# A kernel with a mixture of experts on one core: the experts' work moved into the block before it, and the expert rows weighted, gated and added to the residual rows by the scatter

## What is computed

```python
x = x + gt1 * (merged @ w_out)                    # residual rows x1
h2 = rmsnorm(x, norm2_g) * (1.0 + sc2) + sh2
# each row picks one of 4 groups and 2 of the 8 experts in it; weights: (1024, 2)
y = (silu(h2 @ w1[e]) * (h2 @ w3[e])) @ w2[e]     # for each of its 2 experts e
x = x + gt2 * (weights[:, 0] * y_0 + weights[:, 1] * y_1)     # x2
# second block
h = rmsnorm(x, norm_attn_g_2) * (1.0 + sc1) + sh1
proj = h @ w_in_2
```

## Time and profile before

| what | us |
| --- | --- |
| median of 3 runs | 3923.98 |
| lowest and highest run | 3920.57, 3938.64 |
| the profiled execution | 3928.56 |
| its span, first to last instruction | 3926.7 |
| joining, first to last row of TensorE | 993.3 to 1274.0 |
| experts, first to last row of TensorE | 1290.2 to about 2010.3 |
| mixer, from TensorE's first row | 2024.3 |

### The profile page before, as it was taken

How to read it: one execution, slowest core, us unless ns; L and a number is a source line. 1 busy time by engine, 2 the same in 40 slices (tenths; PEclk the granted TensorE clock), 3 DMA queues, 4 the chain that set the end, 5 groups by cost and what they waited for, 6 DMA issues and landing times. The chain is left out here.

```text
span 3926.7 us, 45778 instructions
## 1 busy us (share of the span) xinstructions
PE 3702.7 (94%) x17988; PEld 1967.0 (50%) x17988; DVE 1739.0 (44%) x2939; ACT 950.9 (24%) x1977; POOL 472.1 (12%) x374
## 2 busy tenths in 40 slices
PE   6999998999998799999968999999898999999999
PEld 3554444555454344444434457865655444444444
DVE  2479998655566000000021335546353344333246
ACT  2311111554232122222223212322243311111001
POOL 0032244311000111111110111111000000000000
PEclk8979999999998899999976999999899999999999
DMA  4213232121554789898955213223103111111334
GB/s 174 75 47 121 76 120 80 55 71 35 207 192 155 278 329 340 329 340 329 341 191 178 101 58 99 79 80 101 60 17 116 41 43 43 43 44 49 125 113 158
DMA packets 295129, 533.07 MB, mean 136 GB/s; under 512 B 25236, under 2 KB 104180, under 8 KB 292638
## 3 DMA queue, kind: packets, MB, share of 16 engines
q1 hardware_dynamic: 277214, 480.56, 35.4%
q0 software_dynamic: 13040, 43.55, 2.8%
q10 hardware_dynamic: 4688, 6.36, 0.4%
HBM read 462.68 MB, written 67.73 MB: 135 GB/s over the span
## 5 line engine op out<-in xcount | busy, mean ns | idle before, releaser
L570 PE MATMUL ch_side<-aT,space 128*128 128x512 f32 x896 | 391.6, 596 | 0.0
L1791 DVE TENSOR_SCALAR ex_y<-ex_y,ex_weight 128x1024 f32<-128x1024 f32 x32 | 41.1, 1284 | 639.9 <-PE ex_y L1711 639.9
L570 PEld LDWEIGHTS ch_side<-aT,space 128*128 128x128 f32 x896 | 168.6, 190 | 213.3 <-issue 210.6
L1695 PE MATMUL ex_a<-space,ex_xT 128*128 128x512 f32 x512 | 229.0, 601 | 6.2 <-ACT ex_xT L1762 6.2
L3015 PE MATMUL en_bank<-en_h,en_up 128*128 128x512 f32 x528 | 233.8, 592 | 0.0
L1711 PE MATMUL ex_y<-aT,ex_actT 128*128 128x512 f32 x512 | 228.1, 599 | 0.7 <-ACT ex_actT L1774 0.7
L1695 PE MATMUL ex_b<-space,ex_xT 128*128 128x512 f32 x512 | 225.0, 592 | 0.0
L2177 PE MATMUL mx_duo<-mx_chunks,mx_region 128*128 128x512 f32 x384 | 183.6, 634 | 0.0
L695 DVE MAX8 ch_best<-ch_score 128x8 f32<-128x384 f32 (+5 forms) x192 | 171.6, 894 | 6.1
L696 DVE MATCH_REPLACE8 ch_score<-ch_best,ch_score 128x384 f32<-128x384 f32 (+5 forms) x192 | 168.1, 875 | 0.0
L1695 PEld LDWEIGHTS ex_a<-space,ex_xT 128*128 128x128 f32 x512 | 98.5, 193 | 130.7 <-issue 130.7
(11 more groups left out here) (536 smaller groups left out, 5884.1 us busy)
## 6 DMA issues: line engine op xcount, KB each, us to landing
space<-exp_w SPq DMA_DIRECT2D x64, 2048.0 KB, 11.8
aT<-exp_w SPq DMA_DIRECT2D x32, 2048.0 KB, 14.0
en_up<-w_down SPq DMA_DIRECT2D x132, 256.0 KB, 3.7
space<-w_ada SPq DMA_DIRECT2D x12, 2048.0 KB, 8.1
mx_x<-proj_padded SPq DMA_DIRECT2D x96, 256.0 KB, 3.6
space<-ada_w SPq DMA_DIRECT2D x8, 2048.0 KB, 8.8
aT<-w_in SPq DMA_DIRECT2D x7, 2048.0 KB, 8.7
en_up<-w_gate SPq DMA_DIRECT2D x22, 512.0 KB, 4.8
```

The lines of the kernel that those rows point to most:

```text
L570: last = nc.tensor.matmul(side_ps[i % 2][:, 0:width], hT[:, k, t * P:(t + 1) * P], by[:, k, 0:width], start=k == 0, stop=k == KD - 1)
L1695: last = nc.tensor.matmul(ps[:, :], xT[b][:, k, :], w13[b][s][:, k, :], start=k == 0, stop=k == KD - 1)
L1791: nc.vector.tensor_scalar(y[b][:, :], y_ps[:, :], weight[b][:, :], None, ALU.mult).then_inc(y_ready, 1)
```

## The change

The functions of `experts` become parts of `joining`'s block: its tiles take memory that `joining` has done with, its PSUM tiles become pairs of `joining`'s banks, and each engine goes on to its experts' work when the new semaphore `listed` says that the experts' list is written. There is no stage boundary between the two any more; `mixer` gets a barrier of all engines at its start. GpSimd also waits for `entered` and `moe_w_stored`. ScalarE issues the store of the weights; the second, small store of it is gone. The first block's `xT` is written half by ScalarE and half by VectorE. gt2 is spread over the partitions at the end of joining (`row2`, `then.gate`), VectorE weights and gates a result in one instruction, and the scatter adds the rows to the x1 rows in HBM (`compute_op=ALU.add`); x2 is the same memory as x1, with 128 more rows for unused places. In `mixer` all work on `ey`, the sums and the stores of x2 are gone. For row tile 1 of joining, VectorE's `weigh("first", 1)` now stands behind `mix(1, 1)`, not ahead of it.

```diff
@@ joining
-        bank = [ctx.enter_context(nc.psum_tensor(f"jn_bank{b}", [P, CH], F32)) for b in range(8)]
+        duo = [ctx.enter_context(nc.psum_tensor(f"jn_duo{b}", [P, 2, CH], F32)) for b in range(4)]
+        bank = [duo[b // 2][:, b % 2, :] for b in range(8)]
...
+        then = experts(nc, g, ctx, space, dsa, aT, duo, gain)
@@ sync
             sp.dma_start(w13[0][1], g.d["exp_w3"][0, 0].rearrange("(k p) f -> p k f", p=P)).then_inc(g.w3_loaded[0], 16)
+            sp.wait_ge(listed, 1)
+            then.sync(sp)
@@ tensor
+            for k in range(KD):
+                column = g.modT[:, 5 * KD + k:5 * KD + k + 1].broadcast_to([P, P])
+                last = nc.tensor.matmul(by_tile(bank[k // 4])[:, k % 4, :], column, g.ident[:, :], start=True, stop=True)
+            last.then_inc(row2, 1)
+            pe.wait_ge(listed, 1)
+            then.tensor(pe)
@@ scalar
+            act.wait_ge(row2, 1)
+            for n in range(2):
+                last = nc.scalar.copy(then.gate[:, n * CH:(n + 1) * CH], bank[n])
+            last.then_inc(then.gate_set, 1)
+            act.wait_ge(weighted, 1)
+            act.dma_start(g.d["moe_w"].rearrange("(t p j) n -> p t (j n)", p=P, j=2), g.weight[:, :, :]).then_inc(moe_w_stored, 16)
+            act.wait_ge(listed, 1)
+            then.scalar(act)
@@ gpsimd
-            pool.wait_ge(weighted, 1)
-            pool.dma_start(g.d["moe_w"][0:SLOTS, :].rearrange("(t p j) n -> p t (j n)", p=P, j=2), g.weight[:, :, :]).then_inc(g.moe_w_stored, 16)
-            pool.dma_start(g.d["moe_w"][SLOTS:SLOTS + P, :], g.eps[:, :]).then_inc(g.moe_w_stored, 16)
+            pool.wait_ge(listed, 1)
+            pool.wait_ge(entered, 1)
+            pool.wait_ge(moe_w_stored, 16)
+            then.gpsimd(pool)
@@ vector
                 mix(t, 0)
-                if t >= 1:
+                if t >= 2:
                     weigh("first", t)
                 mix(t, 1)
-                if t == 0:
+                if t < 2:
                     weigh("first", t)
...
-            chain(V.tensor_copy(g.experts[:, :], line[:, :]))
+            V.tensor_copy(g.experts[:, :], line[:, :]).then_inc(listed, 1)
...
+            chain(TS(g.entries[:, :, 1], target[:, :], -1.0, 0.0, ALU.add, ALU.max))
             chain(TS(blank[:, :], codes, 0.0, empty[:, 0:1], ALU.is_equal, ALU.mult))
-            chain(V.scalar_tensor_tensor(g.entries[:, :, 1], target[:, :], -1.0, blank[:, :], ALU.add, ALU.add))
+            TT(g.entries[:, :, 2], token[:, :], blank[:, :], ALU.add).then_inc(entered, 1)
...
+            dve.wait_ge(listed, 1)
+            then.vector(dve)
@@ experts, now functions that joining calls; what differs in them
+                pool.indirect_dma_start(g.d["x1_rows"], bass.IndirectOffsetOnAxis(entry[b][:, 2:3].bitcast(U32), 0), y[b][:, :], None,
+                                        compute_op=ALU.add).then_inc(scattered[b], 16)
...
+        pe.wait_ge(then.gate_set, 1)
+        pe.wait_ge(x_ready, 1)
+        pe.wait_ge(first_ready, 1)
+        up(0, 0, a_ps, a_done)
...
+        copy_x(1, 0, KD // 2)
...
+        dve.wait_ge(x_flipped, 1)
+        for k in range(KD // 2):
+            last = nc.vector.tensor_scalar(xT[0][:, k, :], x_ps[:, k, :], gain[:, k:k + 1], shift[:, k:k + 1], ALU.mult, ALU.add)
+        last.then_inc(first_ready, 1)
+        dve.wait_ge(then.gate_set, 1)
...
+                nc.vector.scalar_tensor_tensor(y[b][:, :], y_ps, weight[b][:, :], then.gate[:, :], ALU.mult, ALU.mult).then_inc(y_ready, 1)
@@ mixer
+    nc.all_engine_barrier()
...
-                y_v = g.d["moe_y"][0:SLOTS, :].rearrange("(t p j) n -> p t j n", p=P, j=2)
-                for t in range(NT + 2):
+                for t in range(NT):
+                    yield -20.0 if t < 2 else N3_PACE * (t - 2) + 2.0
                     if t >= 2:
-                        yield N3_PACE * (t - 2) - 0.1
-                        sp.wait_ge(combined, t - 1)
-                        sp.dma_start(rows(g.d["x2"])[:, t - 2, :], nx[t % 2]).then_inc(x2_stored[t % 2], 16)
-                    if t < NT:
-                        yield -20.0 if t < 2 else N3_PACE * (t - 2)
-                        sp.dma_start(ey[t % 2], y_v[:, t, :, :]).then_inc(e_loaded[t % 2], 16)
-                        if t >= 2:
-                            yield N3_PACE * (t - 2) + 2.0
-                            sp.wait_ge(n_scaled, t - 1)
-                            sp.wait_ge(x2_stored[t % 2], 16 * (t // 2))
-                        sp.dma_start(nx[t % 2], rows(g.d["x1"])[:, t, :]).then_inc(n_loaded[t % 2], 16)
+                        sp.wait_ge(n_scaled, t - 1)
+                    sp.dma_start(nx[t % 2], rows(g.d["x2"])[:, t, :]).then_inc(n_loaded[t % 2], 16)
...
-                    act.wait_ge(combined, t + 1)
+                    act.wait_ge(n_loaded[t % 2], 16 * (t // 2 + 1))
...
-                    nc.gpsimd.tensor_tensor(ey[t % 2][:, 0, :], ey[t % 2][:, 0, :], ey[t % 2][:, 1, :], ALU.add).then_inc(e_paired, 1)
...
-                    chain(TT(ey[t % 2][:, 0, :], ey[t % 2][:, 0, :], e_gate, ALU.mult))
-                    TT(nx[t % 2], nx[t % 2], ey[t % 2][:, 0, :], ALU.add).then_inc(combined, 1)
@@ program
-        d["x1"], d["x2"] = scratch("x1", (S, D)), scratch("x2", (S, D))
+        d["x1_rows"] = scratch("x1_rows", (S + P, D))
+        d["x1"] = d["x2"] = d["x1_rows"][0:S, :]
```

363 lines of the change are left out of this document (164 added, 199 removed).

## The result

The changed kernel takes 3913.72 us in the median (3907.53 to 3916.49), the kernel before 3928.15 us (3920.57 to 3938.64) beside it. These are six executions of seven; the seventh took 7612.73 us, about twice as long, for a reason that no profile shows, and is left out of all numbers. The ratio is 0.9957, with a 95% interval of 0.9938 to 0.9975: 14 us less by the medians, 10 to 24 by the interval. The forecast was 3910.5 us in a range of 3896 to 3926, and "same" within 0.5%.

A forecast was written before the change was run, and what follows sets the result against it. TensorE, busy for 94% of the span, was taken to bound the kernel. Terms 3.4 - 11.6 + 0 + 0.5 + 0.9 - 6.7 = -13.5 us took the median from 3923.98 to 3910.5 us, range 3896 to 3926.

The forecast's parts named there:

- A, the order: Joining's row tile 1, weigh behind mix: wait and slow work come back at flip_x(0), +3.4 us, bounds -6.8 and +4.5.
- B, no boundary: Joining to experts: first w1 product starts at 1283.75 instead of 1295.35, -11.6 us, bounds -12.4 and -9.4.
- count from the last issue: End of experts: the drain may count from GpSimd's last DMA issue, ending 10.2 to 10.6 us after it, hiding the landing.
- C, the loop: Experts' loop: combined weighting and accumulating scatter cost no time, 0 us, with the DMA share below 0.97.
- The bound from rows: Experts' loop: an accumulating scatter takes some 2.6 us, as a plain scatter plus a gather of the same size.
- D, the end of experts: End of experts: +0.5 us for the last scatter and drain, +0.9 us for the added barrier.
- E, the mixer's head: Mixer's start: first square 3.9 us after the stage's begin, not 9.9, and a 0.70 us wait gone; -6.7 us.
- The reordering: Faster rival in joining: an early second load pulls flip_x(0) forward, part worth -6.8 us, time 3900.3 us; chance 0.12.
- The mixer's head start: Rival: a later mixer wait eats it and weights crowd the first gather, +6.7 + 2.2 us, 3919.4 us; chance 0.16.
- The accumulating scatter: Slower rival in the experts' loop: it makes DMA the bound, +53 us over 31 blocks, 3963 us; chance 0.10.
- My deciding point: Experts' loop: DMA becomes the bound once an accumulating scatter takes over 3.5 us of the 16 engines.

The follow-up runs named there:

- after: The changed kernel itself, with all parts of the change to the kernel before: 3913.72 us in the median, ratio 0.9957.
- Experiments 2 and 3: Changed kernel with joining's boundary put back, 3915.5 us; then also GpSimd issuing the 8 KB store, 3905.21 us; then also the tiny store, 3917.62 us.
- plain_scatter: Changed kernel with the scatter as a plain write, leaving out the residual rows: 3910.82 us, ratio 0.996.
- mixer_alone: Kernel before with only the mixer's part of the change, the experts' contribution left out: 3927.24 us, ratio 0.9989.
- scatter_twice: Changed kernel with a second accumulating scatter in each block, to a spare tensor: 3913.96 us, ratio 0.9964.
- before: The kernel without the change, 3928.15 us in the median; profiled a second time unchanged, 3937.24 us in one execution.
- order_back: Changed kernel with the new order in joining's row tile 1 undone: 3905.01 us, ratio 0.9947.
- scatter_four: Changed kernel with four accumulating scatters in each block instead of one, three to spare tensors: 4085.72 us in one execution.

## Why the prediction was right, step by step

**A, the order: predicted +3.4, measured +2.2 in after and +2.9 on the mean of seven profiles with the new order (283.4 against 280.5 in the four without it or idle work, and no profile of the one lies among the other).** The steps held: the idle time ahead of flip_x(0) was to be some 7 us and is 7.35; the slow work was to come back and did. Only the product behind flip_x(0) was quicker than in the earlier trace rows, 7.95 us and not 8.97.

**B, no boundary: predicted -11.6, measured -11.4.** The number was right, and one step under it was wrong. Landing was taken as 5.1 us and was 5.3; transposes, halves and handovers came as worked out, with the first product 9.09 us behind the gather (8.87 predicted). But the prediction took the gain for one boundary's, and in D it used joining's drain as one of two cases in which a drain may count from the last issue; at joining's end it ended with the last landing. Experiments 2 and 3 split the 11.4 us otherwise: 4.0 the boundary, 0.6 the 8 KB store's place on GpSimd's queue, 5.5 the tiny store that is no longer made, and the rest, 1.3 to 1.5, goes to the scaling in halves on two engines (TensorE's wait for it is 1.79 us and not 3.14 as in the earlier trace rows). By this split, half of the gain lay in one store of 512 bytes; the kernel before without that store alone was not run.

**C, the loop: predicted 0, measured 0 (plain_scatter, 713.25 against 712.95 us; mixer_alone, with the old loop, 712.63).** The bound from rows, 2.6 us for an accumulating scatter, is what was measured: queue 0 went from 11.9% to 17.9%, 1.3 us of a block on top of the plain scatter's 1.3, and the second one of scatter_twice added 12 points more, 2.6 us. The DMA share was to be 0.92 to 0.97 and is 0.96. The Trainium skill, "Collectives: The Full Stack", section "Stop ④ — SDMA + CCE: where bytes move and the add happens", has the adder read both operands and write once; that the scatter's time doubles, from 1.3 to 2.6 us, agrees. GpSimd's issue grew from 0.99 to 1.59 us, which nobody waits for.

**D, the end of experts: predicted +1.4, measured +0.7.** The last landing grew from 3.4 to 6.2 us, more than the 1.3 us that reading as well was to add, and the drain hid all of it: it was to take about 8 us again and took 4.9, ending 11.4 us behind the issue's start as against 11.6 before. What is left is the barrier (scatter to load is 11.9 to 13.1 us in the others that have it, 17.5 with four scatters): 0.97 us from the block's last event at 2016.8 to the load, 0.9 predicted from the earlier trace rows.

**E, the mixer's head: predicted -6.7, measured -7.2 up to the first wide product** (6.3 from load to square, 0.9 from square to wide). The prediction put the rest of the mixer at nothing, holding it for full. From wide to ending, though, another 2.3 and 5.3 us are gone against the two profiles of before, and 5.2 between the means (923.5 in those two, 918.3 in the eleven with the new mixer and no idle work in it; these lie between 910.6 and 924.9). The window of the earlier trace rows that showed TensorE busy throughout began at 2180. Ahead of it, from a narrow product of line 2124 (2139 after) to the first of the table sums, stand before, after and scatter_twice, which has the new mixer as well:

```profile
2085.90:2166.96 81.06, 70.12 (x180) 37.22 (x179) 16.56 (x20) 28.73 (x66) 10.33 (x4) 0.71 0.41 148
```

```profile
2071.92:2148.28 76.36, 66.06 (x179) 34.46 (x178) 7.80 (x14) 28.67 (x66) 3.30 (x1) 0.75 0.20 69
```

```profile
2073.90:2155.16 81.26, 70.05 (x179) 37.23 (x178) 7.81 (x14) 28.67 (x66) 3.30 (x1) 0.71 0.19 64
```

The same work of TensorE takes 76.4 us in after and not 81.1, at a granted clock of 0.75 and not 0.71, with VectorE busy 7.8 us and not 16.6, GpSimd 3.3 and not 10.3, and half the DMA share. But scatter_twice, with as little work beside TensorE as after, takes 81.3 us at 0.71. So the lighter load beside TensorE does not by itself shorten this stretch; its length goes with the clock. It was 81.1 and 80.9 us in the two profiles of before, and 76.2 to 78.3 us at 0.74 or 0.75 in ten of the eleven with the new mixer. Whether the change makes the better clock likelier, or two profiles of before are too few to tell, is open.

**The sum.** A to E give 2.2 - 11.4 + 0 + 0.7 - 7.2 = -15.7 us, against -13.5 predicted and -14.4 between the medians. The profiles say more, 2933.4 - 2912.1 = 21.3 us from J0 on, and the difference is 4.1 us from up to scatter (3.0 of them the last down product's clock) and 2.3 us of the mixer behind wide, again a matter of the clock, less 0.8 in the last stage. That the median agrees so well with the sum is in part luck: what the clock adds from run to run is of the size of the terms. The executions of the kernel before alone lie 18 us apart. By the times only the whole is clear; the parts are read from stretches, most of them of one profile each. In time the forecast of 3910.5 us was 3.2 us low: its base, the median of three executions, was 4.2 us under the median of seven.

**The rivals.** The reordering did not keep its gain (order_back). The mixer's head start was not eaten in the profile of mixer_alone; its times, 4.3 us with an interval from 8.6 to a loss of 0.4, leave that less sure. The accumulating scatter did not bind, and scatter_twice shows that even twice of it, 5.2 us, does not. My deciding point, 3.5 us, was too low: it took a share of 1.0 for full, and 1.05 is, and the weights' packets took less of it beside two scatters.

## What to carry to other kernels

Before a boundary is blamed for its length, read the landing of every transfer that GpSimd has issued ahead of its drain: one 512-byte store, put back, cost 5.5 us here and the boundary itself 4.0. A wait taken from TensorE is paid only when the next engine's chain can follow; the time TensorE then idles can also cost it its clock. Idle matmuls that fit the gap can give that back, in some runs; their time is to be read first (48 of float32 took 10.88 us here). Compare profiles by stretches between the same instructions, know how well each stretch repeats, and profile the kernel before more than once.

## What the runs showed of the hardware that I had not expected

- A GpSimd store of 128 rows of 4 bytes landed 9.9 to 10.1 us after its issue in all four profiles that have it, while 8 KB issued just before it landed in 5.5 to 6.3.
- At joining's end GpSimd's drain ended 0.8 to 0.9 us behind the last landing, in six of six. At the experts' end a drain of 4.9 us followed a scatter that landed in 6.2 us, one of 8.4 us a scatter that landed in 3.3; the two ends lie 11.4 and 12.0 us behind the issue's start, and neither follows the landing.
- The queues' shares of the DMA engines sum to 1.05 where they are full. The loop runs at that share without any wait of TensorE in scatter_twice, with w1 and w3 landing in 18.8 us instead of 11.0; in scatter_four, where they land in 32.0 us, TensorE waits.
- An 8 KB store that ScalarE issued beside the weights' loads took 13.4 us to land, against the 5.5 to 6.3 of the same store on GpSimd ahead of a boundary; GpSimd waited 15 us for it in after, and nobody waited for GpSimd.
- With the same code in the mixer, after and scatter_twice differ by 4.9 us in a stretch of 80 us. TensorE's idle time in it is 10.3 and 11.2 us; the other 4.0 us are slower work, at a granted clock of 0.71 instead of 0.75.
